# Hybrid decoder layer: w_mod in three column parts, h modulated on ScalarE and split on VectorE

## What the kernel computes

```
mod = silu(c) @ w_mod + b_mod                   # w_mod: 2048 x 12288
sh1, sc1, g1, sh2, sc2, g2 = split(mod, 6)
h    = rms_norm(x, norm1_w) * (1 + sc1) + sh1   # 1024 x 2048
proj = h @ w_in                                 # columns: a, g, z, xbc, dt
u    = causal_conv31(a * sigmoid(g))            # then group norm and silu
```

## Time and profile before

| | |
|---|---|
| median of three runs | 3262.5 us |
| the profiled execution's own time | 3264.45 us |
| its span in the trace | 3262.8 us |
| mean granted clock of TensorE in the span | 0.929 |
| busy: TensorE, VectorE, ScalarE, GpSimd | 87%, 76%, 46%, 18% |
| first block: to the end of output tile 0 | 206.4 us of the span |

### The profile page before, as it was taken

One profiled execution on the slowest core, in us unless ns is written; L12 is line 12 of the kernel. 1 busy time (PEld: TensorE's weight loads), 2 busy tenths in 40 slices (PEclk: granted clock), 3 DMA queues, 4 the chain that ended last, 5 costly groups with the idle time before them and its releaser, 6 DMA issues. The chain is left out here.

```text
span 3262.8 us, 36512 instructions
## 1 busy us (share of the span) xinstructions
PE 2833.7 (87%) x12749; PEld 2292.8 (70%) x12749; DVE 2464.7 (76%) x1827; ACT 1499.0 (46%) x1234; POOL 573.5 (18%) x444
## 2 busy tenths in 40 slices
PE   2699999999996767899964899999999999999970
PEld 2577777777874655677854788878887788778850
DVE  5977888876545993678645788888888888888859
ACT  4122222212112331000031788888888888878852
POOL 0210000000003553455500111111111111111100
PEclk7799999999998888999965899999999999999985
DMA  8712112225521115777762798999888999899968
GB/s 311 260 39 69 53 57 71 58 60 171 163 69 52 48 33 192 234 222 245 230 246 116 287 363 361 376 383 377 355 354 353 394 395 364 355 375 381 379 247 369
DMA packets 248421, 771.98 MB, mean 237 GB/s; under 512 B 25176, under 2 KB 119432, under 8 KB 179516
## 3 DMA queue, kind: packets, MB, share of 16 engines
q1 hardware_dynamic: 185618, 613.76, 49.7%
q10 hardware_dynamic: 50810, 115.73, 10.3%
q0 software_dynamic: 11952, 41.97, 3.2%
HBM read 733.62 MB, written 82.84 MB: 250 GB/s over the span
## 5 line engine op out<-in xcount | busy, mean ns | idle before, releaser
L1915 DVE TENSOR_TENSOR wlo<-wraw,whi 128x2048 fp32r<-128x2048 f32 x444 | 1006.4, 2288 | 181.6 <-ACT whi L1864 181.5
L1864 ACT ACTIVATE whi<-wraw 128x2048 fp32r<-128x2048 f32 x444 | 843.4, 1916 | 245.0 <-PE ps L1849 115.3
L1795 PE MATMUL ps<-whi,xhi 128*128 128x512 f32 x1184 | 475.2, 401 | 0.0
L1797 PE MATMUL ps<-whi,xlo 128*128 128x512 f32 x1184 | 462.9, 391 | 0.0
L1796 PE MATMUL ps<-wlo,xhi 128*128 128x512 f32 x1184 | 462.2, 390 | 0.0
L358 PE MATMUL ps<-hh,wih 128*128 128x512 f32 x1152 | 372.2, 404 | 27.6 <-POOL hl L310 18.7
L358 PE MATMUL ps<-hl,wih 128*128 128x512 f32 x1152 | 363.9, 397 | 0.0
L358 PE MATMUL ps<-hh,wil 128*128 128x512 f32 x1152 | 362.9, 396 | 0.0
L657 DVE SCALAR_TENSOR_TENSOR acc<-u,vcur,acc 128x1024 f32<-128x1024 f32 x240 | 308.3, 1285 | 7.7
L358 PEld LDWEIGHTS ps<-hh,wih 128*128 128x128 f32 x1152 | 217.8, 190 | 90.2 <-POOL hl L310 19.5
L333 ACT ACTIVATE wih<-wraw_i 128x1024 fp32r<-128x1024 f32 x72 | 76.1, 1057 | 401.6 <-PE ps L358 317.0
(11 more groups left out here) (327 smaller groups left out, 4394.5 us busy)
## 6 DMA issues: line engine op xcount, KB each, us to landing
wraw<-in_w_gate_dram SPq DMA_DIRECT2D x148, 1024.0 KB, 6.8
wraw<-in_w_up_dram SPq DMA_DIRECT2D x148, 1024.0 KB, 7.6
wraw<-in_w_down_dram SPq DMA_DIRECT2D x148, 1024.0 KB, 7.6
slot<-in_w_mod_dram ACTq DMA_DIRECT2D x96, 512.0 KB, 4.8
wraw_i<-in_w_in_dram SPq DMA_DIRECT2D x72, 512.0 KB, 3.9
wmA<-in_w_mod_dram SPq DMA_DIRECT2D x48, 512.0 KB, 5.6
wraw_o<-in_w_out_dram SPq DMA_DIRECT2D x64, 256.0 KB, 4.4
y<-ybuf_d SPq DMA_DIRECT2D x16, 1024.0 KB, 12.1
```

The lines of the kernel that those rows point to most:

```text
L1795: pe.matmul(dst, xhi[:, t, :], whi[:, s, w], start=(t == 0), stop=False)
L1797: last = pe.matmul(dst, xlo[:, t, :], whi[:, s, w], start=False, stop=(t == KT - 1))
L1864: act.activation(whi[:, spl(m), :], wraw[:, raw(m), :], ACT.Copy).then_inc(s_whi, 1)
L1915: dve.tensor_tensor(wlo[:, spl(m), :], wraw[:, raw(m), :], whi[:, spl(m), :].bitcast(F32), ALU.subtract).then_inc(s_wsp[raw(m)], 1)
```

## The change

What it does, engine by engine:

- w_mod's columns come in three parts instead of two: those of h tiles 0 to 7 (1024 columns each for sh1 and sc1, 32 pieces as before), of tiles 8 to 11 and of tiles 12 to 15 (512 columns each; one DMA brings both, so 16 pieces of 512 KB a part, which VectorE takes as two products of 128x512). Slots are wmA's four and two in wmB instead of four.
- VectorE makes all subtractions hl = h - hh (`split_h`), ScalarE all modulations (an Identity activation with sc1 and sh1 as column scale and bias). GpSimd keeps only its two memsets, which wait for the first columns.
- ScalarE scales x tiles 4 to 7, between its copies of tiles 0 to 3 out of PSUM; VectorE scales 0 to 3. VectorE's first two products on w_mod stand ahead of the second reciprocal.
- TensorE makes tile 0 in three parts: over tiles 0 to 7, 8 to 11 and 12 to 15, each for r = 0, 1, 2. The columns of the next part stand between r = 1 and r = 2 of a part.
- The splits of w_in's pieces (three for each half) stand between products of w_mod.

```
+    PARTS = ((0, KT // 2), (KT // 2, 3 * KT // 4), (3 * KT // 4, KT))
 SP
+    for t in range(KT):
+        for v in range(2):
+            dst, m, turn = wm_piece(0, t, v)
+            if turn > 0:
+                sp.wait_ge(s_mv[v], t - 1)
+            sp.dma_start(dst, wm2_v[:, t, v * D:v * D + 1024]).then_inc(s_wm[m], 16)
+        if t in (KT // 2, KT // 2 + 2, KT // 2 + 4):
+            first((t - KT // 2) // 2)
+    for part in (1, 2):
+        for t in range(KT):
...
+            sp.dma_start((wmA, wmB)[m // 4][:, m % 4, :].rearrange("p (v n) -> p v n", v=2),
+                         wm2_v[:, t, 0:2 * D].rearrange("p (v n) -> p v n", v=2)[:, :, c0:c0 + 512]
+                         ).then_inc(s_wm[m], 16)
+        if part == 1:
+            for k in range(3, 6):
+                first(k)
 GpSimd
-    for t in range(KT):
-        if not by_vector(t):
-            pool.wait_ge(s_mh, t + 1)
-            pool.tensor_tensor(hl[:, t, :], htmp[t % 3][:], hh[:, t, :].bitcast(F32),
-                               ALU.subtract).then_inc(s_hlp, 1)
+    pool.wait_ge(s_mcol, 1)
 TensorE
+    mod_columns(0)
+    for part in range(3):
+        for r in range(3):
+            if r == 2 and part < 2:
+                mod_columns(part + 1)
+            first_proj(pe, r, part)
 ScalarE
+    # in the loop over j, for j < 4, ahead of the copies of x tile j
+    i = TT // 2 + j
+    act.wait_ge(s_rst, 2)
+    act.activation(xin[:, i, :], xin[:, i, :], ACT.Copy, scale=rstd[:, i:i + 1]).then_inc(s_xna, 1)
...
+    def modulate(t):
+        if t >= 3:
+            act.wait_ge(s_hl, t - 2)
+        act.activation(htmp[t % 3][:], hT[:, t, :], ACT.Identity, scale=sc1[:, t:t + 1],
+                       bias=sh1[:, t:t + 1]).then_inc(s_mt, 1)
+    for part, (t0, t1) in enumerate(PARTS):
+        act.wait_ge(s_mods, 3 * part + 3)
+        modulate(t0)
+        for t in range(t0, t1):
+            if t + 1 < t1:
+                modulate(t + 1)
+            round_h(t)
+        for k in ((3,), (4, 5), ())[part]:
+            round_w(act, k, 0)
 VectorE
+    rstd_x(0)
+    dve.wait_ge(s_rst, 1)
+    for j in range(TT // 2):
+        dve.tensor_scalar(xin[:, j, :], xin[:, j, :], rstd[:, j:j + 1], None, ALU.mult).then_inc(s_xn, 1)
     dve.wait_ge(s_cact, 1)
+    mod_piece(0, 0)
+    rstd_x(1)
+    for t in range(1, KT):
+        mod_piece(0, t)
+        if t >= KT - 3:
+            split_w(dve, t - (KT - 3), 0)
...
+    mod_piece(1, 0)
     mods(0)
+    for t in range(0, KT // 2):
+        mod_piece(1, t + 1)
+        split_h(t)
+    for t in range(KT // 2 + 1, KT):
+        mod_piece(1, t)
+    split_w(dve, 3, 0)
+    mod_piece(2, 0)
+    mods(1)
+    for t in range(4):
+        mod_piece(2, 1 + t)
+        split_h(KT // 2 + t)
+    for t in range(5, KT):
+        mod_piece(2, t)
+        if t == 7:
+            split_w(dve, 4, 0)
+    split_w(dve, 5, 0)
+    mods(2)
+    for t in range(12, KT):
+        split_h(t)
```

More of the change, by code:

```diff
@@ L345, in proj @@
                         s = (2 * r + q) % 3
[L346 to L351 removed]
+                        pe.wait_ge(s_wsp[s], 2 * it + (2 * r + q) // 3 + 1)
                         for k in range(8):
                             t = 8 * q + k
[L354 to L355 removed]
                             for n, (w, x_) in enumerate(((wih, hh), (wih, hl), (wil, hh))):
@@ L361, in proj, with first_proj @@
                         last.then_inc(s_wu[s], 1)
+                def first_proj(pe, r, part):
+                    t0, t1 = PARTS[part]
+                    pe.wait_ge(s_wsp[r], t0 // 8 + 1)
+                    for t in range(t0, t1):
+                        pe.wait_ge(s_hl, t + 1)
+                        for n, (w, x_) in enumerate(((wih, hh), (wih, hl), (wil, hh))):
+                            for h in range(2):
+                                last = pe.matmul(ps[:, 1024 * r + 512 * h:1024 * r + 512 * h + 512], w[:, r, t % 8, :],
+                                                 x_[:, t, 512 * h:512 * h + 512],
+                                                 start=(t == 0 and n == 0), stop=(t == KT - 1 and n == 2))
+                    if t1 % 8 == 0:
+                        last.then_inc(s_wu[r], 1)
                 def stat(pe, src, done):
@@ L381, in _ @@
                     for j in range(TT):
-                        pe.wait_ge(s_xn, j + 1)
+                        if j < TT // 2:
+                            pe.wait_ge(s_xn, j + 1)
+                        else:
+                            pe.wait_ge(s_xna, j - TT // 2 + 1)
                         for q in range(4):
@@ L736, in mods, with mod_piece @@
-                    def mods(half):
-                        cols = slice(half * (KT // 2), (half + 1) * (KT // 2))
-                        dve.wait_ge(s_mcol, half + 1)
+                    def mod_piece(part, t):
+                        for v in range(2):
+                            src, m, turn = wm_piece(part, t, v)
+                            dve.wait_ge(s_wm[m], 16 * turn + 16)
+                            if t == 0:
+                                ins = dve.tensor_scalar(macc(part, v), src, cact[:, 0:1], None, ALU.mult)
+                            else:
+                                dve.wait_ge(s_mv[v], KT * part + t)
+                                ins = dve.scalar_tensor_tensor(out=macc(part, v), in0=src, scalar=cact[:, t:t + 1],
+                                                               in1=macc(part, v), op0=ALU.mult, op1=ALU.add)
+                            ins.then_inc(s_mv[v], 1)
@@ L739, in mods @@
+                    def mods(part):
+                        cols = slice(*PARTS[part])
+                        dve.wait_ge(s_mcol, part + 1)
                         for v, dst in enumerate((sh1, sc1)):
-                            ins = dve.tensor_tensor(dst[:, cols], ps[:, 3584 + v * KT + cols.start:3584 + v * KT + cols.stop],
-                                                    colv[:, v, cols], ALU.add)
-                            ins.then_inc(s_mods, 1)
-                        dve.wait_ge(s_mods, 3 * half + 2)
+                            dve.tensor_tensor(dst[:, cols], ps[:, 3584 + v * KT + cols.start:3584 + v * KT + cols.stop],
+                                              colv[:, v, cols], ALU.add).then_inc(s_mods, 1)
+                        dve.wait_ge(s_mods, 3 * part + 2)
```

140 lines of the change are left out of this document (37 added, 103 removed).

## The result

The changed kernel took 3235.8 us (median of four runs, 3230.8 to 3242.9), beside 3260.7 us of the kernel before in the same comparison: ratio 0.9928, interval 0.9914 to 0.9942. A second, longer comparison gave 3237.7 against 3258.9, ratio 0.9937 [0.9922, 0.9953]. The forecast was 3241, its range 3233 to 3254, and "faster" with 0.84. The profiled execution took 3242.88 us (span 3241.3); the sum made against the profiled execution of before had given 3243.1. That these two agree to 0.2 us is luck: another execution of the same kernel, profiled in the second comparison, took 3232.89 us.

The account below looks back on a forecast made before the run. TensorE's loop was taken as the bound, so tile 0's gain carries through: 109.3 - 93.0 = 16.3 us from T on, with the earlier w_mod stream (5.0) 21.3 us, from 3262.5 to 3241 us; range 3233 to 3254.

Parts of the forecast that it names:

- What bounds: TensorE alone bounds the loop behind tile 0, so finishing tile 0 earlier moves all that follows by as much.
- mark: End of tile 0's third projection, where ScalarE is let go: 206.45 us before, predicted at T + 93.0 instead of T + 109.3.
- The stream: Loading and multiplying w_mod ahead of T: starts earlier, gain 5.0 us (bounds 0 and 6.1), with 0.3 deducted for splits.
- T: The moment of the first modulated tile of h: 97.1 us before, predicted at 92.1 us.
- Scaling on ScalarE: Four tiles of x, 7.8 us on ScalarE, claimed to cost nothing under TensorE's wait; up to 8 us without that cover.
- Part 0: Tiles 0 to 7: VectorE sets a step of 2.46 us a tile instead of 4.07; r=1 done at T+34.4.
- rival of a low clock: 48 matmuls of r=1 or r=2 over tiles 0 to 7 cost 9.4 us more at half clock: 3250 us, chance 0.16.
- table load: ScalarE loads a table of 1.28 us at each turn between Copy and Identity, two a tile: 3278 us, chance 0.06.
- Part 1 and the new wait: Tiles 8 to 11: TensorE waits 5 us for VectorE ahead of the third columns, then runs 5.6 us at half clock.
- Part 2 and what lasts: Tiles 12 to 15 end at T+93.0; the first convolution, 48.6 us, then fits with 1.4 us over.
- transfers bind: Pieces of w_mod take 1.68 us instead of 1.32, ending 4 us later; with no stream gain 3250 us, chance 0.09.
- all is taken back: Tile 0's gain is lost to the first convolution or a loop wait: within 0.2% of 3262 us, chance 0.08.

Follow-up runs that it names:

- head undone: Changed kernel with all x scaling back on VectorE, ahead of the first w_mod product: 3244.5 us, ratio 0.9954 to the kernel before.
- VectorE modulates: Changed kernel with the modulation of h back on VectorE, which also still subtracts: 3245.7 us, ratio 0.9961 to the kernel before.
- two halves: Changed kernel with w_mod in two halves instead of three parts, second columns behind r=2 of the first half: 3242.8 us, ratio 0.9955.
- GpSimd in part 0: Changed kernel with the subtractions of h tiles 0 to 7 back on GpSimd, ScalarE still modulating: 3244.3 us, ratio 0.9967.
- kept busy: Changed kernel with twenty matmuls nobody reads ahead of the third columns, so TensorE does not idle: 3233.9 us, ratio 0.9939.
- four parts: Changed kernel with four parts of four h tiles each instead of three parts: 3238.0 us, ratio 0.995 to the kernel before.
- the change again: The changed kernel without any edit, timed in a second comparison: 3237.7 us, ratio 0.9937 to the kernel before.
- waits filled: Changed kernel, VectorE's queue only reordered: more products ahead of its waits, w_in splits behind part 0's last product: 3233.2 us, ratio 0.9923.
- four filled: Changed kernel with four parts of four tiles and VectorE's waits filled with products, later w_in splits moved back: 3227.6 us, ratio 0.990.
- columns last: Changed kernel with the next part's columns behind r=2 instead of between r=1 and r=2: 3253.6 us, ratio 0.999 to the kernel before.
- head alone: Kernel before with only the new head: ScalarE scales half of x, first two products ahead of the second reciprocal: 3256.6 us, ratio 0.9999.
- splits behind: Changed kernel with only the three w_in splits moved behind the last product of part 0: 3234.4 us, one run.

## Why the prediction was right, step by step

**What bounds.** Right: tile 0 decided all. The mark also prices the experiments. Against the kernel before in the same comparison, mark and median moved by 15.3 and 15.1 us (head undone), 16.0 and 14.0 (VectorE modulates), 14.5 and 16.8 (two halves), 15.3 and 12.7 (GpSimd in part 0), 22.5 and 23.2 (kept busy), 20.4 and 19.1 (four parts), 20.4 and 21.2 (the change again), 28.0 and 25.7 (waits filled), 29.8 and 31.3 (four filled). These agree to 2.6 us, and so does columns last (3.5 and 6.0); only head alone falls out, with 4.5 and 0.4.

**The stream.** The first product stands at 32.19 (32 to 33 predicted). T is 92.88 where 92.1 was predicted: the gain is 4.2, not 5.0. The term that was too small is the one for the splits between the last products, 0.3. I had reasoned that VectorE has 10 us of gaps in this stretch. It has (10.5 us of waiting for pieces up to the columns), but they lie ahead: from 75.66 us on there is no gap, and what is put there comes out at the end. With the splits taken out, "splits behind" has its columns at 84.66, 5.0 us ahead of the earlier trace rows, where the sum had 5.3 before its deduction of 0.3; against the two executions of the change the splits cost 0.6 to 1.2 us. In head alone, whose splits also stand behind, the columns come at 85.66, a microsecond later; half of this is there at the first product (32.56 against 32.04), the rest no run explains.

**Scaling on ScalarE** cost nothing that the runs show, by the cover that the prediction named: the first columns wait 26.7 us for the stream.

**Part 0.** The step of a tile is 2.46 us (96.23 to 98.69), as summed up. A modulation takes 1.24 us (1.25 taken, 1.06 the other end), a pair of half-wide products 1.41. The second columns start at 127.32, T + 34.4, the number of the prediction. Its rival of a low clock is refuted by the window 103 to 115 us, granted 1.00 with TensorE busy 8.36 of 12; it stays at 1.00 up to the third columns. The table load is refuted by ScalarE's rows: its sixteen modulations alternate with roundings, and no load of 1.28 us stands between them. The rule of the Trainium skill weighed in the prediction (ScalarE: Activation LUTs, "Table sets: the hidden batching unit") holds here for Identity as for Copy.

**Part 1 and the new wait.** 4.87 us (5 predicted) and columns at half clock in 3.54 (3.5). Behind them the low clock lasted until 164.4 us, 3.5 us where 5.6 were taken, and this is why T to mark took 92.1 us and not 93.0. In this execution two errors, 0.8 too little and 0.9 too much, cancel: that the mark came within 0.1 us of the predicted one is luck. In the second execution the low clock lasted about 5 us, and T to mark took 92.7:

```profile
161.00:167.00 6.00, 6.00 (x18) 4.81 (x18) 1.62 (x4) 5.06 (x5) 0.00 (x0) 0.55 0.19 57
```

So the term is not so much mis-sized as different from execution to execution; in "splits behind" it was nearly 6 us. A wait of 0.88 us for the fifth split had been put at 1.0.

**Part 2 and what lasts.** The first u at 179.44 (179.5), the next after 1.35 us of waiting (1.4 over): the first convolution just fits. "Two rows of 2 KB are no bound" held but for one wait of 2.5 us, behind which VectorE still stood 0.7 us for the columns, so the rival "transfers bind" is out. With TensorE busy in 70.00 of 70.00 us behind tile 0, the rival that all is taken back is out too.

**What it did not say.** From T on the pace was VectorE's, in a stage whose waits I had read on TensorE only. The prediction named VectorE at each step, but not as the engine that has to be kept fed. The 2.04 us ahead of the first subtraction and the 4.03 ahead of the factors are in the trace as VectorE's idle time, with landed pieces behind them, and filling them gave 6.6 to 7.6 us at the mark by a mere reordering. The reading of TensorE's waits was also one line short: the 6.3 us for VectorE's low parts stand in the same view. The expectation for four parts made the same mistake again: it moved T by 29 us and put VectorE's work behind it too low (all pieces through near 140 to 146, when the fourth columns came at 158.03).

**How much of a median is luck.** Between the two profiled executions of the change lie 10 us that the mark does not show (184.99 in the one of 3242.88 us, 186.05 in the one of 3232.89). They arise far behind: the first matmul of the experts starts at 1814.9 us in one and at 1806.4 in the other. In the stage before it the windows differ in the granted clock. First the execution of 3242.88 us, then that of 3232.89:

```profile
1650.00:1675.00 25.00, 22.95 (x118) 21.75 (x118) 9.78 (x5) 8.83 (x16) 1.07 (x2) 0.57 0.38 152
...
1650.00:1675.00 25.00, 22.89 (x146) 22.10 (x145) 11.88 (x6) 8.61 (x16) 1.06 (x2) 0.73 0.49 201
```

TensorE is busy for the same 23 of 25 us, but gets through 118 matmuls in one and 146 in the other. The clock goes with the time in the other runs too: 55 runs of the kernel before lie between 3246 and 3268 us, those with a mean clock of 0.929 at 3261 to 3266, those with 0.935 at 3246 to 3249. That it is the cause was looked at in these two executions only. The first comparison shows 24.9 us, 3.4 more than the mark; the second 21.2. The difference may be this. So the four runs of the first comparison (two near 3231, two above 3240) cannot tell a prediction of 3241 from one of 3236.

## What to carry to other kernels

Where a result is computed in parts that each need a round trip between engines (sums, columns, factors, tiles), put the round trip ahead of the last work of the part before: here undoing it alone made tile 0 18 us longer, the other edits 4 to 7 each, and three parts with an open round trip were 11 us worse than two. Then look for the engine whose step sets the pace and fill *its* waits with work that has already arrived, before adding more parts: a reordering gave about as much (6.6 to 7.6 us) as the third part with its early columns had (6.9), and a fourth part without it gave nothing. Work is free in an engine's gaps only if gaps are left behind it; in the last microseconds ahead of the point that others wait for, an instruction can cost up to its full time: two splits of 1.1 us made the columns 2.0 us later in one kernel, and between 0.6 and 1.2 in another.

## What was not expected of the hardware

- Two engines that share no semaphore held each other up one instruction against one: a 128x512 product on VectorE stretched from 0.75 to 2.8 us while GpSimd subtracted 128x1024 in 2.83 us, itself slower than the 2.35 of before. I had expected a slow-down of the one or the other, not the exact alternation.
- The granted clock fell to half from about 161 to 164 us although twenty matmuls had been put into the gap ahead, and TensorE stood still for 0.34 us only. The sixteen column products before it, each one column wide, took 1.92 us.
- The clock that one program gets near 1650 us differs from execution to execution (0.57 or 0.73 in the same window of 25 us); in the two executions looked at, 8.5 of the 10 us between them were there when the experts began, right behind that stage.
